# Tiles, exponentials and transfers of the mLSTM stage put in another order

## The chip, the cores and the metric

The kernel runs on one core of one Trainium2 chip. The time is the device time of one execution in microseconds (us). The program starts five instruction streams: PE (TensorE, the matmuls), DVE (VectorE), ACT (ScalarE), POOL (GpSimd) and SP (SyncE, which here only issues DMA transfers). They run at the same time and meet only at semaphores, so the time is set by whichever chain of work and waits is longest.

## The reference, cut to what matters

The program is two blocks of two layers each on 512 latent and 256 context tokens of 1024 features (768 tokens in all), in float32. The change lies in the first layer of the first block, an mLSTM mixer with 8 heads, run over chunks of 128 tokens in both directions:

```python
d = b[..., :, None] - b[..., None, :] + li[..., None, :]
d = jnp.where(jnp.tril(jnp.ones((L, L), dtype=bool)), d, -jnp.inf)
inter = b + m0[..., None]
m_t = jnp.maximum(jnp.max(d, axis=-1), inter)
wq = jnp.exp(d - m_t[..., None]) * jnp.einsum("bhctd,bhcsd->bhcts", q_c, k_c)
carry_w = jnp.exp(inter - m_t)
num = jnp.einsum("bhcts,bhcse->bhcte", wq, v_c) + carry_w[..., None] * jnp.einsum("bhctd,bhcde->bhcte", q_c, c0)
den = jnp.sum(wq, axis=-1) + carry_w * jnp.einsum("bhctd,bhcd->bhct", q_c, n0)
h = num / jnp.maximum(jnp.abs(den), jnp.exp(-m_t))[..., None]
```

Before it the tokens are projected to queries and keys, values, output gates and scan gates. Beside it every layer needs a modulation vector, `silu(c) @ ada_w + ada_b`, for the latents and for the context: 48 tiles of `ada_w` for this layer, of which the first 16 are done by matmuls at the start and the other 32 beside the projections.

## The kernel before, in words

**Weight stream.** All weights are read as tiles of 128x1024 floats (512 KB). `weight_plan` lists them in one order. SP loads tile i into one of three stage buffers; it waits until the tile three places earlier has been used up. A projection tile is then split into a rounded part and a remainder: `W.hi` lets ACT write the rounded part (L195), `W.lo` lets DVE subtract it (L209, `wlo`). There are four pairs of such parts, so ACT may round tile n+4 only when PE has used tile n. PE takes a tile in 24 matmuls of 512 and 24 of 256 columns, with the rounded part, the rounded part again against the remainder of the tokens, and the remainder. A modulation tile (`ada0`) takes no PE: DVE multiplies it with a spread conditioning vector (`CB0`, two of them) and sums, in two passes (L491), and only then is its stage buffer free. Where modulation tiles stand in the plan thus decides when DVE does these passes: it works in the order of the plan.

**The projections of this layer.** In the order of the plan: 1 tile of scan gates (`mgate`), 8 of queries and keys (`mqk`), 8 of values (`mv`, in two groups of four), 8 of output gates (`mo`), 8 of the output (`mout`). The results lie in four slots of PSUM, used in turn. A group of `mv` fills three slots and claims all three before its first matmul; ACT and DVE empty them (`mV`, L899 and L1018), DVE after the tiles that stand in the plan up to its place. After the first `mqk` tiles DVE works out the scans of the gates (L973 to L1009), some 25 us in one piece.

**The mixer.** Heads are taken in four pairs p = 0 to 3, each in two directions d. The names used below are those of the code:

- `spread_max(p)` is two DMA issues of ACT's queue that spread the rows of running maxima over 128 partitions, into `mD` (the tiles mDD[p][0] and mDD[p][1], 768 KB each). mDD[1] and mDD[3] share one place, the second half of `Ht`; `CB0` lay in that place too.
- `bands(p)` is two POOL instructions (L1138) that subtract the causal mask in `mD`.
- `decay(p, d)` is 12 exponentials of ACT over `mD` (L860), then DVE `weights(p, d)` multiplies the scores of PSUM into it (L1026).
- `spread_reach(p)` is four DMA issues (192 KB each) into `mRQ`; `ends(p)` copies the chunk ends to `mG` on ACT (L868); `reach(p)` is two POOL multiplications with the queries (L1145).
- PE: `keys` (turns the keys), `scores`, `states` (key-value products), `within(p, d)` (inside a chunk), `past(p, d)` (from the carried state; it waits for `reach(p)` and for DVE's state chain at L1056 and L1060).
- `sizes(p, d)` on ACT takes the absolute value of the denominators (`mDN`, L919) after `past(p, d)`; DVE `normalise(p, d)` takes their maximum with the floor (L1068), the reciprocal (L1070) and scales the result into `mH` (L1079 for d=0, L1085 for d=1); ACT `squares` and DVE `head_norm` (L1095) follow.

PE does, for each p: within(p,0), past(p,0), keys(p+1), within(p,1), past(p,1), the turning of the former pair, scores(p+1), states(p+1,0), states(p+1,1). The scores of the next pair need the PSUM slots that the result of direction 1 holds, so they wait for DVE's last L1085 of this pair.

Two orders are written out by hand and matter here: ACT's in the loop over p, and POOL's list of bands and reaches.

## Time and profile before

| what | value |
|---|---|
| median of 3 runs | 3561.91 us (3559.08 to 3564.73) |
| profiled execution | 3561.91 us, its span in the trace 3560.2 us |
| PE busy | 3242.3 us, 91% of the span |
| DVE, ACT, POOL busy | 1881.3, 1170.2, 208.9 us |
| DMA | 318.73 MB, mean 90 GB/s |

The span is the time from the first to the last instruction in the trace; 1.7 us of the profiled execution lie around it. The chain of the page is the work that ended last, followed back step by step. The mLSTM layer takes the first tenth: its projections run from 80 to 307 us, its pairs from 307 to 405 us.

### The profile page before, as it was taken

To read this page: it belongs to the slowest core of one execution; us is meant where nothing else is said; L and a number is where in the kernel's file an instruction comes from. 1 tells how busy PE (TensorE), PEld (TensorE's weight loads), DVE (VectorE), ACT (ScalarE), POOL (GpSimd) and SP (SyncE) were. 2 spreads that over 40 slices of the span, in tenths; PEclk is the share of its full clock that TensorE was granted. 3 is DMA by queue.
4 is the path that set the end of the run, shared out by engine and by line. 5 is a ranking of instruction groups with operands and counts; after the bars stand their busy time and mean duration, and the time that the engine had idled before them with its cause. 6 is when DMAs were issued, how large, how long until landed. Compare 5 with 4: busy or idle time off the path is not lost.

```text
span 3560.2 us, 44175 instructions
## 1 busy us (share of the span) xinstructions
PE 3242.3 (91%) x18456; PEld 2699.3 (76%) x18456; DVE 1881.3 (53%) x2747; ACT 1170.2 (33%) x1757; POOL 208.9 (6%) x144
## 2 busy tenths in 40 slices
PE   8998889999989779999998999988998888997997
PEld 8877778888877667777777878756887777775776
DVE  2765646655434664777454342574434544456543
ACT  3315331212232554222342333253212534425322
POOL 0002100000010000000001220000001012000001
PEclk9999999999989999999999999999999799989997
DMA  4454113333212002555221123102122222310321
GB/s 177 136 180 146 45 48 126 123 130 119 95 54 70 3 1 95 177 177 177 95 93 70 64 71 113 42 1 80 54 72 89 76 68 86 112 58 9 100 87 59
DMA packets 90926, 318.73 MB, mean 90 GB/s; under 512 B 10006, under 2 KB 11926, under 8 KB 89960
## 3 DMA queue, kind: packets, MB, share of 16 engines
q1 hardware_dynamic: 81348, 288.91, 24.5%
q10 hardware_dynamic: 9380, 26.99, 2.1%
q8 instruction: 147, 2.41, 0.3%
q14 instruction: 51, 0.42, 0.0%
HBM read 294.12 MB, written 21.74 MB: 89 GB/s over the span
## 4 chain that ended last, share of the span: by engine, by line
PE 78%; DVE 10%; ACT 8%; issue 4%; DMA 0%; ACTq 0%; POOL 0%; POOLq 0%; DVEq 0%; SPq 0%
PE PS L384 77%; ACT whi L195 2%; ACT Pq L1246 1%; DVE STs L1283 1%; PE PS L387 1%; ACT nt L588 1%; DVE JUNK L491 1%; DVE stage L491 1%; DVE STq L1283 1%; ACT Ps L1246 1%; DVE wlo L209 1%; ACT U L593 0%; DVE fg L693 0%; ACT Ht L2276 0%; ACT FS L1637 0%
## 5 line engine op out<-in xcount | busy, mean ns | idle before, releaser
L384 PE MATMUL PS<-U,whi 128*128 128x512 f32 (+1 forms) x5408 | 1176.7, 363 | 89.3 <-DVE U L613 24.1
L384 PEld LDWEIGHTS PS<-U,whi 128*128 128x128 f32 x5408 | 912.3, 192 | 278.0 <-issue 54.1
L209 DVE TENSOR_TENSOR wlo<-stage,whi 128x1024 fp32r<-128x1024 f32 x339 | 417.6, 1233 | 1107.8 <-ACT whi L195 1107.2
L195 ACT ACTIVATE whi<-stage 128x1024 fp32r<-128x1024 f32 x339 | 358.4, 1058 | 1459.3 <-PE PS L384 1424.5
L384 PE MATMUL PS<-U,wlo 128*128 128x512 f32 (+1 forms) x2704 | 621.4, 356 | 0.0
L384 PE MATMUL PS<-Y,whi 128*128 128x512 f32 (+1 forms) x2240 | 581.7, 363 | 18.3 <-DVE Y L695 12.2
L384 PEld LDWEIGHTS PS<-U,wlo 128*128 128x128 f32 x2704 | 458.5, 190 | 80.0
L384 PEld LDWEIGHTS PS<-Y,whi 128*128 128x128 f32 x2240 | 396.5, 191 | 93.1 <-DVE Y L695 14.2
L384 PE MATMUL PS<-Y,wlo 128*128 128x512 f32 (+1 forms) x1120 | 367.2, 362 | 0.0
L384 PE MATMUL PS<-whi,U 128*128 128x512 f32 (+2 forms) x832 | 237.2, 374 | 11.3 <-DVE mV L1018 6.4
L384 PEld LDWEIGHTS PS<-Y,wlo 128*128 128x128 f32 x1120 | 208.6, 190 | 34.9
L384 PEld LDWEIGHTS PS<-whi,U 128*128 128x128 f32 x832 | 158.5, 206 | 39.9 <-issue 11.9
L491 DVE CUSTOM_DVE_ANT_0 JUNK<-stage,CB,CL 128x1024 f32<-128x1024 f32 x128 | 163.7, 1279 | 0.5 <-DMA stage<-in_ada 0.4
L491 DVE CUSTOM_DVE_ANT_0 stage<-stage,CB,CL 128x1024 f32<-128x1024 f32 x128 | 164.0, 1281 | 0.0
L384 PE MATMUL PS<-wlo,U 128*128 128x512 f32 (+2 forms) x416 | 155.2, 373 | 0.0
L528 POOL TENSOR_TENSOR ACC<-ACC,SQ 128x768 f32<-128x768 f32 (+1 forms) x24 | 37.6, 1567 | 1356.3 <-ACT SQ L521 1356.3
L675 ACT ACTIVATE Y<-fg 128x768 fp32r<-128x768 f32 (+1 forms) x64 | 47.3, 739 | 207.7 <-DVE fg L693 207.7
L384 PEld LDWEIGHTS PS<-wlo,U 128*128 128x128 f32 x416 | 85.9, 206 | 12.8
L1246 ACT ACTIVATE Pq<-PS,STq 128x768 f32<-128x768 f32 (+1 forms) x80 | 65.1, 815 | 86.8 <-DVE STq L1287 67.8
L2312 POOL TENSOR_TENSOR ACC<-ACC,Ht 128x768 f32<-128x768 f32 (+1 forms) x14 | 21.8, 1561 | 1101.8 <-DVE Ht L2294 1101.8
L695 DVE TENSOR_TENSOR Y<-fg,Y 128x768 fp32r<-128x768 f32 (+1 forms) x64 | 52.8, 826 | 51.6 <-ACT Y L675 51.6
L1283 DVE TENSOR_REDUCE STq<-PS 128x1 f32<-128x768 f32 (+1 forms) x80 | 67.6, 845 | 16.9 <-PE PS L384 15.6
(408 smaller groups left out, 3329.3 us busy)
## 6 DMA issues: line engine op xcount, KB each, us to landing
stage<-in_w SPq DMA_DIRECT2D x128, 512.0 KB, 3.3
stage<-in_ada SPq DMA_DIRECT2D x80, 512.0 KB, 3.3
stage<-in_adb SPq DMA_DIRECT2D x48, 512.0 KB, 3.3
stage<-in_p_mg SPq DMA_DIRECT2D x16, 512.0 KB, 3.3
stage<-in_p_ma SPq DMA_DIRECT2D x16, 512.0 KB, 3.4
stage<-in_p_ms SPq DMA_DIRECT2D x16, 512.0 KB, 3.4
stage<-in_wo SPq DMA_DIRECT2D x16, 512.0 KB, 3.3
GS<-FS ACTq DMA_DIRECT2D x20, 384.0 KB
```

The costliest lines, as they stand in the source:

```text
L195: act.activation(self.parts[r % n][0], self.stage[i % len(self.stage)], ACT.Copy).then_inc(*self.S.up("w_hi", i))
L209: dve.tensor_tensor(lo, self.stage[i % len(self.stage)], hi.bitcast(F32), ALU.subtract).then_inc(*self.S.up("w_lo", i))
L384: return pe.matmul(o, l, r, start=start, stop=stop_, skip_group_check=True)
L387: return pe.transpose(o, i, IDENT[0:k, 0:k])
L491: dve.tensor_tensor_reduce(tile if v else JUNK, tile, CB[n][v], 1.0, col(("ada2_b" if b else "ada_b") + str(L), t), ALU.mult, ALU.add, MOD ...
L528: pool.tensor_tensor(ACC[:, 0:N], ACC[:, 0:N], SQ[k % 2][:, 0:N], ALU.add).then_inc(*up("sq_add", r, k))
L588: ins = act.activation(a[:, lo:hi], a[:, lo:hi], ACT.Identity, bias=mod(L, ish, k, v), scale=MU[:, 8 * v + k:8 * v + k + 1])
L675: act.activation(Y[:, 0, k, 0:N], FB[n % 2][:, 0:N], ACT.Copy).then_inc(*up("f_hi", L, g, k))
L695: dve.tensor_tensor(Y[:, 1, k, 0:N], b, Y[:, 0, k, 0:N].bitcast(F32), ALU.subtract).then_inc(*up("f_lo", L, g, k))
L1246: act.activation(a.P[n % 2][:, h, 0:c], B.of(("a_s", a.tag, n, h))[:, 0:c], ACT.Exp, bias=nm[:, h:h + 1], scale=0.125, accum_out=sm[:, h:h ...
L1283: dve.tensor_reduce(mx[:, h:h + 1], B.of(("a_s", a.tag, n, h))[:, 0:c], AX.X, ALU.max).then_inc(*up("a_max", a.tag, n, h))
L2312: pool.tensor_tensor(ACC[:, 0:N], ACC[:, 0:N], HT[:, k, 0:N], ALU.add).then_inc(*up("e_add", L, k))
```

## The change: what it does

1. `weight_plan`: the 32 modulation tiles stand earlier. Before, one stood behind each of `mqk` 3 to 7, two behind an `mv` tile (one behind the fourth and the eighth), and 13 among the `mo` tiles. Now two stand behind each of `mqk` 3 to 7 and behind each `mv` tile, and two behind each of `mo` 0 to 2; behind `mo` 3 to 7 none.
2. `CB0` lies in another place, under the last output gates (`mO` 5 to 7). So the second half of `Ht` is free as soon as the normalisation has read it, and `spread_max(1)` is issued right behind `spread_max(0)`, between the two groups of `mv`; the eviction of `mo` 5 waits for the last modulation tile.
3. ACT, `mqk` and `mo`: the rounding of a coming tile (`W.hi`) stands ahead of the eviction of the tile just projected.
4. ACT, exponentials: both directions of a pair stand together, for pair 0 behind `mo` 4, for pair p+1 between `sizes(p, 0)` and `ends(p + 1)`; before, direction 1 stood behind `sizes(p, 1)`.
5. POOL: `bands(3)` stands ahead of `reach(2)`.

```diff
--- before.py
+++ after.py
@@ -260,13 +260,13 @@
     add("mgate", [0])
     for j in range(8):
         add("mqk", [j])
-        ada(1 if j >= 3 else 0)
+        ada(2 if j >= 3 else 0)
     for j in range(8):
         add("mv", [j])
-        ada(1 if j % 4 == 3 else 2)
+        ada(2)
     for j in range(8):
         add("mo", [j])
-        ada(2 if j < 6 else 7 - j)
+        ada(2 if j < 3 else 0)
     add("mout", range(8))
     for L in range(2):
         if L:
@@ -435,7 +435,7 @@
 
 
         CB = [[place(f"CB{n}{v}", [128, 1024], F32, o + 4096 * v)[:, :] for v in range(2)]
-              for n, o in enumerate((offH + 12288, offZ + 16384, offZ + 16384))]
+              for n, o in enumerate((offY2 + 16384, offZ + 16384, offZ + 16384))]
         FIRST = [place(f"first{g}", [128, 2, 1024], F32, (offU + 8192 * g) if g < 6 else offY + 8192 * (g - 6))
                  for g in range(8)]
         JUNK = place("JUNK", [128, 1024], F32, offZ + 34848)[:, :]
@@ -851,14 +851,15 @@
                         *dma(f"m_rin{p % 2}", p, d, h))
 
         def act_mlstm(act):
-            def decay(p, d):
-                act.wait_ge(*at("m_band", p, d))
-                for h in range(2):
-                    r = m_row(p, h, d)
-                    for c in range(6):
-                        x = mDD[p][d][:, h, 128 * c:128 * c + 128]
-                        ins = act.activation(x, x, ACT.Exp, bias=maT[:, c, r:r + 1], scale=-1.0)
-                    ins.then_inc(*up("m_dx", p, h, d))
+            def decay(p):
+                for d in range(2):
+                    act.wait_ge(*at("m_band", p, d))
+                    for h in range(2):
+                        r = m_row(p, h, d)
+                        for c in range(6):
+                            x = mDD[p][d][:, h, 128 * c:128 * c + 128]
+                            ins = act.activation(x, x, ACT.Exp, bias=maT[:, c, r:r + 1], scale=-1.0)
+                        ins.then_inc(*up("m_dx", p, h, d))
 
             def ends(p):
                 act.wait_ge(*at(f"m_rin{p % 2}", p, 1, 1))
@@ -875,10 +876,10 @@
             act.activation(mTM[r40, :], mTM[r40, :], ACT.Ln).then_inc(*up("m_gexp", 1))
             for j in range(8):
                 i = T("mqk", j)
+                W.hi(act, i)
                 act.wait_ge(*at("w_used", i))
                 act.activation(mQK[:, j, :], B.of(i)[:, 0:TOK], ACT.Copy, scale=1.0 if j < 4 else 0.125).then_inc(
                     *up("m_qk", j))
-                W.hi(act, i)
             act.wait_ge(*at("m_rows"))
             act.activation(mRR[r40, :], mRR[r40, :], ACT.Exp, scale=-1.0).then_inc(*up("m_reach"))
             act.dma_start(mROWS[0, :, :], mMR[r40, :]).then_inc(*dma("m_spill", 0))
@@ -900,18 +901,19 @@
                                    rows_of(("mv", g), c, 512).rearrange("p (h e) -> p h e", e=128), ACT.Copy).then_inc(
                                        *up("m_va", g, c))
                 if g == 0:
+                    act.wait_ge(*at("n_mul", 0, 7))
                     act.wait_ge(*at("m_spill", 1))
                     spread_max(act, 0)
+                    spread_max(act, 1)
             for j in range(8):
                 i = T("mo", j)
+                W.hi(act, i)
                 act.wait_ge(*at("w_used", i))
+                if j == 5:
+                    act.wait_ge(*at("mod", T("ada0", 47), 1))
                 act.activation(mOT[:, j, :], B.of(i)[:, 0:TOK], ACT.Sigmoid).then_inc(*up("m_o", j))
-                W.hi(act, i)
-                if j in (3, 4):
-                    decay(0, j - 3)
-                if j == 6:
-                    act.wait_ge(*at("mod", T("ada0", 47), 1))
-                    spread_max(act, 1)
+                if j == 4:
+                    decay(0)
 
             def sizes(p, d):
                 act.wait_ge(*at("m_av", p, d))
@@ -939,11 +941,9 @@
             for p in range(4):
                 sizes(p, 0)
                 if p < 3:
-                    decay(p + 1, 0)
+                    decay(p + 1)
                     ends(p + 1)
                 sizes(p, 1)
-                if p < 3:
-                    decay(p + 1, 1)
                 if p < 2:
                     spread_reach(act, p + 2)
                 if p == 1:
@@ -1138,20 +1138,16 @@
                     pool.tensor_tensor(x, x, CM[:, 384 + 128 * d:512 + 128 * d].unsqueeze(1).to_broadcast([128, 12, 128]),
                                        ALU.subtract).then_inc(*up("m_band", p, d))
 
-            def reach(p):
+            bands(0)
+            bands(1)
+            for p in range(4):
                 for d in range(2):
                     x = mRQ[p % 2][d]
                     pool.wait_ge(*at("m_g", p, d))
                     pool.tensor_tensor(x, x, mQK[:, p, :], ALU.mult).then_inc(*up("m_q", p, d))
-
-            bands(0)
-            bands(1)
-            reach(0)
-            bands(2)
-            reach(1)
-            reach(2)
-            bands(3)
-            reach(3)
+                if p in (0, 1):
+                    bands(p + 2)
+
 
 
 
@@ -2375,7 +2371,7 @@
             for L in range(2):
                 act_norm_mod(act, 2 * L, L, 0, True)
                 if L == 0:
-                    act_spread(act, 0, ("n_mul", 0, 7))
+                    act_spread(act, 0)
                     act_mlstm(act)
                 else:
                     act_swa(act)
```

In the order of ACT's instructions the loop over the pairs shows points 4 and 2. Below is pair 0 and the start of the next step, before the change; mD10 and mD11 are the tiles of pair 1 in direction 0 and 1, mG the ends, mDN the sizes, mRQ the reach, mJ the squares.

```order
L919 ACTIVATE mDN_108<-PS 128x6 x2
L860 ACT_TABLE_LOAD
L860 ACTIVATE mD10_118<-mD10_118,maT_105 128x128 x12
L868 ACTIVATE mG_110<-mRQ10_127 128x6
L868 ACTIVATE mG_110<-mRQ11_128 128x6
L919 ACTIVATE mDN_108<-PS 128x6 x2
L860 ACTIVATE mD11_119<-mD11_119,maT_105 128x128 x12
L850 DMA mRQ00_125<-mROWS 64x768 x2
L850 DMA mRQ01_126<-mROWS 64x768 x2
L929 ACTIVATE mJ_124,mSQ_109<-mH00_135 128x128 x6
```

And the same place of ACT after the change:

```order
L921 ACTIVATE mDN_108<-PS 128x6 x2
L861 ACT_TABLE_LOAD
L861 ACTIVATE mD10_118<-mD10_118,maT_105 128x128 x12
L861 ACTIVATE mD11_119<-mD11_119,maT_105 128x128 x12
L869 ACTIVATE mG_110<-mRQ10_127 128x6
L869 ACTIVATE mG_110<-mRQ11_128 128x6
L921 ACTIVATE mDN_108<-PS 128x6 x2
L850 DMA mRQ00_125<-mROWS 64x768 x2
L850 DMA mRQ01_126<-mROWS 64x768 x2
L931 ACTIVATE mJ_124,mSQ_109<-mH00_135 128x128 x6
```

The twelve exponentials of direction 1 have moved from behind the second mDN to ahead of it, and ahead of both mG. The same holds for pairs 2 and 3.

POOL's list from the reach of pair 0 on, before (mRQ00 and mRQ01 serve pairs 0 and 2, mRQ10 and mRQ11 pairs 1 and 3; mD2 and mD3 are the bands of pairs 2 and 3):

```order
L1145 TENSOR_TENSOR mRQ00_125<-mRQ00_125,mQK_100 128x768
L1145 TENSOR_TENSOR mRQ01_126<-mRQ01_126,mQK_100 128x768
L1138 TENSOR_TENSOR mD20_120<-mD20_120,CM_60 128x1536
L1138 TENSOR_TENSOR mD21_121<-mD21_121,CM_60 128x1536
L1145 TENSOR_TENSOR mRQ10_127<-mRQ10_127,mQK_100 128x768
L1145 TENSOR_TENSOR mRQ11_128<-mRQ11_128,mQK_100 128x768
L1145 TENSOR_TENSOR mRQ00_125<-mRQ00_125,mQK_100 128x768
L1145 TENSOR_TENSOR mRQ01_126<-mRQ01_126,mQK_100 128x768
L1138 TENSOR_TENSOR mD30_122<-mD30_122,CM_60 128x1536
L1138 TENSOR_TENSOR mD31_123<-mD31_123,CM_60 128x1536
```

After the change, from the reach of pair 1 on:

```order
L1147 TENSOR_TENSOR mRQ10_127<-mRQ10_127,mQK_100 128x768
L1147 TENSOR_TENSOR mRQ11_128<-mRQ11_128,mQK_100 128x768
L1138 TENSOR_TENSOR mD30_122<-mD30_122,CM_60 128x1536
L1138 TENSOR_TENSOR mD31_123<-mD31_123,CM_60 128x1536
L1147 TENSOR_TENSOR mRQ00_125<-mRQ00_125,mQK_100 128x768
L1147 TENSOR_TENSOR mRQ01_126<-mRQ01_126,mQK_100 128x768
```

The two mD3 instructions now stand ahead of the reach of pair 2 instead of behind it.

On DVE the place between the two groups of `mv` shows point 1. Before, from the remainder of the eighth `mv` tile (wlo_53) to the emptying of PSUM:

```order
L209 TENSOR_TENSOR wlo_53<-stage_50,whi_52 128x1024
L491 ISA JUNK,MOD_63<-stage_51,CB_73,CL 128x1024
L491 ISA MOD_63 128x1
L491 ISA stage_51,MOD_63<-stage_51,CB_74,CL 128x1024
L491 ISA MOD_63 128x1
L1018 COPY mV<-PS 128x4x128 x3
```

After:

```order
L209 TENSOR_TENSOR wlo_53<-stage_50,whi_52 128x1024
L491 ISA JUNK,MOD_63<-stage_51,CB_73,CL 128x1024
L491 ISA MOD_63 128x1
L491 ISA stage_51,MOD_63<-stage_51,CB_74,CL 128x1024
L491 ISA MOD_63 128x1
L491 ISA JUNK,MOD_63<-stage_49,CB_73,CL 128x1024
L491 ISA MOD_63 128x1
L491 ISA stage_49,MOD_63<-stage_49,CB_74,CL 128x1024
L491 ISA MOD_63 128x1
L1018 COPY mV<-PS 128x4x128 x3
```

One modulation tile more stands between that remainder and the copy.

## Rows read from the trace of the kernel before

**Rows 1.** The page, shares of the chain that ended last, by engine

```profile
PE 78%; DVE 10%; ACT 8%; issue 4%; DMA 0%; ACTq 0%; POOL 0%; POOLq 0%; DVEq 0%; SPq 0%
```

**Rows 2.** Waits of the first 700 us: total us, times, longest us

```profile
PE PS L384 <- DVE mH L1085: 12.0, 3, 5.7
```

**Rows 3.** Windows: length, busy per engine (instructions), TensorE clock, DMA share, GB/s

```profile
330.25:337.40 7.15, 6.63 (x64) 6.16 (x64) 3.49 (x8) 3.74 (x17) 3.36 (x2) 0.60 0.42 104
378.50:383.80 5.30, 3.96 (x64) 3.60 (x64) 5.16 (x10) 4.96 (x25) 0.00 (x0) 1.00 0.02 3
```

**Rows 4.** Timeline (start, duration, instruction, [idle before]): DVE, end of the gate scans

```profile
123.98 1.22 DVE L209 TENSOR_TENSOR wlo<-stage,whi 128x1024 fp32r<-128x1024 f32 x1
```

**Rows 5.** Timeline of PE: start of the fifth mqk tile, start of mv

```profile
127.49 3.90 PE L384 MATMUL PS<-U,whi 128*128 128x512 f32 x16
...
162.43 0.50 PE L384 MATMUL PS<-whi,U 128*128 128x512 f32 x1
```

**Rows 6.** Timeline of ACT: the rounding behind the last mqk eviction

```profile
162.00 1.05 ACT L195 ACTIVATE whi<-stage 128x1024 fp32r<-128x1024 f32 x1
```

**Rows 7.** Timeline of DVE between the two groups of mv

```profile
198.61 1.28 DVE L491 CUSTOM_DVE_ANT_0 JUNK<-stage,CB,CL 128x1024 f32<-128x1024 f32 x1
...
201.13 1.89 DVE L1018 COPY mV<-PS 128x512 f32<-128x512 f32 x3
```

**Rows 8.** Timeline of PE: start of the second group of mv

```profile
202.70 1.19 PE L384 MATMUL PS<-whi,U 128*128 128x512 f32 x2 [6.42 <-DVE mV L1018]
```

**Rows 9.** Timeline of all engines, from the last projection to pair 0

```profile
304.95 6.86 POOL L1138 TENSOR_TENSOR mD<-mD,CM 128x1536 f32<-128x1536 f32 x2 [91.92 <-DMA mD<-mROWS]
...
308.97 3.92 DVE L209 TENSOR_TENSOR wlo<-stage,whi 128x1024 fp32r<-128x1024 f32 x1 [3.73 <-ACT whi L195]
...
312.76 1.08 ACTq L844 DMA_DIRECT2D mD<-mROWS  x2
...
313.89 0.31 ACT L868 ACTIVATE mG<-mRQ 128x6 f32<-128x6 f32 x2 [4.96 <-DMA mRQ<-mROWS]
313.90 2.42 PE L384 MATMUL PS<-mV,mKH 128*64 128x129 f32 x40 [3.43 <-DVE mKH L1044]
...
317.24 1.39 PE L384 MATMUL PS<-mS,mRQ 64*128 64x129 f32 x20 [0.92 <-DVE mS L1060]
```

**Rows 10.** Timeline of all engines, pair 0

```profile
320.22 3.62 ACT L860 ACTIVATE mD<-mD,maT 128x128 f32<-128x128 f32 x12
...
323.24 6.82 POOL L1138 TENSOR_TENSOR mD<-mD,CM 128x1536 f32<-128x1536 f32 x2 [5.47 <-DMA mD<-mROWS]
...
324.64 0.24 ACT L919 ACTIVATE mDN<-PS 128x6 f32<-128x6 f32 x2 [0.60 <-PE PS L384]
...
324.92 1.79 DVE L1068 TENSOR_TENSOR mDN<-mDN,meT 128x12 f32<-128x12 f32 x1 [0.96 <-ACT mDN L919]
...
327.01 3.19 DVE L1085 SCALAR_TENSOR_TENSOR mH<-PS,mDN,mH 128x128 f32<-128x128 f32 x12
```

**Rows 11.** Timeline of all engines, pair 1

```profile
348.09 1.30 DVE L1068 TENSOR_TENSOR mDN<-mDN,meT 128x12 f32<-128x12 f32 x1 [0.96 <-ACT mDN L919]
348.10 0.45 ACTq L850 DMA_DIRECT2D mRQ<-mROWS  x1
...
350.53 0.60 ACTq L844 DMA_DIRECT2D mD<-mROWS  x1
```

**Rows 12.** Timeline of all engines, pair 2

```profile
359.77 7.58 POOL L1138 TENSOR_TENSOR mD<-mD,CM 128x1536 f32<-128x1536 f32 x2 [8.65 <-DMA mD<-mROWS]
...
362.80 1.39 PE L384 MATMUL PS<-mS,mRQ 64*128 64x129 f32 x20
...
369.58 3.57 POOL L1145 TENSOR_TENSOR mRQ<-mRQ,mQK 128x768 f32<-128x768 f32 x2 [2.22 <-ACT mG L868]
...
374.52 0.24 ACT L919 ACTIVATE mDN<-PS 128x6 f32<-128x6 f32 x2 [4.92 <-PE PS L384]
...
378.52 1.61 PE L384 MATMUL PS<-mQK 64*128 64x128 f32 x24 [2.59 <-DVE mH L1085]
```

## The prediction

> **What bounds the kernel now.** I read the page's chain first [rows 1]: TensorE ends last and carries 78% of the chain, so a change counts only where it makes PE wait or stop waiting, plus the clock PE is granted. Next the waits of the first 700 us, the part that the change touches. Among the pairs PE's largest waits are for DVE's last scaling of a pair's result, three in all [rows 2]: scores of the next pair need its PSUM. Third, the timeline between 94 and 405 us. The projections leave PE almost no idle time; the one large gap is 6.42 us between the two groups of value tiles [rows 8]. The pairs are a tight ring PE, ACT, DVE, POOL, in which nearly any delay reaches PE. So I sum the gaps place by place, in the profiled execution's own time, which is the median itself: 3561.91 us. After the mixer the work is the same, and a shift carries through.
>
> **Queries and keys.** Behind the fourth tile stand two modulation tiles instead of one, and DVE does both before the 25 us of scans. A tile costs DVE 2.4 to 2.5 us (198.61 to 201.13) [rows 7]. The next remainder starts at 123.98 and lasts 1.22 [rows 4]; with 2.4 more it ends at 127.6, PE wants it at 127.49 [rows 5]: +0.2 us (bounds 0 and 1). Later tiles have DVE work of 1.2 + 2 x 2.4 = 6.1 us per tile against PE's 8.4 (127.49 to 135.9), so the lag closes.
>
> **Rounding ahead of eviction.** The rounding, 1.05 us, began at 162.00 right behind the last mqk eviction [rows 6]; now it precedes it, and the eviction ends near 163.1. The first value group claims the slot it frees and began at 162.43 [rows 5]: +0.7 us (0 to 1). Elsewhere four slots give a tile's eviction at least 8 us of slack, which covers 1 us.
>
> **Between the value groups.** DVE empties PSUM behind one modulation tile, now behind two: the gap of 6.42 us becomes 8.8. The tile's load has landed, since its buffer came free early. +2.4 us, bounds 2.3 and 2.6. It is the surest term.
>
> **Last projection to pair 0.** What speaks for the change is here. POOL's bands for pair 1 ran 304.95 to 311.8, because CB0 held their memory until late; DVE's remainder at 308.97 took 3.92 us instead of 1.2, it ended 1.1 us after POOL, and PE lost 3.43 us [rows 9]. With the bands a hundred us earlier that cover is gone, and something else is late next: mG comes at 313.89, after its DMA issues, and DVE's state chain and POOL's reach both wait for it. The chain then takes 0.2 + 0.3 + 1.5, PE can do past(0,0) near 316.1 instead of 317.24 [rows 9]. So -1.1 us, not -3.4 (the bounds: 0 if the mout load, which now comes earlier, delays the reach transfers; -3.4 if mG is not late). The moved bands may hold DVE at 213 to 221 us; cover is the remainder it then makes, for a tile that PE takes 20 us later.
>
> **Pair 0.** ACT now does 24 exponentials ahead of sizes(0,1). Twelve take 3.62 [rows 10]. From past(0,0) at 317.5: 0.3 sizes, 1.3 table, 7.2 exponentials, 0.3 mG, so sizes(0,1) ends at 326.8; before it was 324.9 [rows 10]. Then comes the maximum at L1068, two operands in SBUF. Before, it was issued at 324.92 while POOL ran the first band, and took 1.79 us, until that band ended at 326.63: it waits for the POOL instruction that is running. Now it is ready when the second band runs. That band ended at 330.06 [rows 10] and will end some 1.3 us earlier, because the mout load no longer shares its transfer: 328.8. Scaling starts at 329.2 instead of 327.01, and scores(1) at +2.2 against before, a term of +3.3 over the -1.1. Bounds: +1.2 if DVE slips in free, +4.6 if the band ends as before. I take the middle since pair 3's transfer, with no mout load beside it, let POOL start 9.2 us after its issue (350.53 to 359.77) [rows 11, 12], pair 2's 10.5 us after (312.76 to 323.24) [rows 9, 10].
>
> The Trainium skill, "SBUF — State Buffer", section "SBUF: two separate sides", says that DVE with two SBUF inputs and a GpSimd instruction exclude each other for the whole instruction, and that whoever starts first holds the ports. The row of 1.79 us agrees. By that rule DVE's modulation passes would be held beside the moved bands too, which no row of before shows; it would change nothing in the sum as long as the 20 us above hold.
>
> **Pair 1.** The same exponentials put sizes(1,1) 3.5 us later against the rest of the pair. Before, L1068 lost 1.30 us at 348.09 to POOL's reach(2) [rows 11]; that reach now comes later and this loss goes. Net 3.5 less 1.2 to 1.3: +2.3 us (bounds 1.5 and 3.6).
>
> **Pair 2.** POOL does bands(3) before reach(2). bands(3) can't start before their transfer lands, 359.77, and end at 367.4 [rows 12]. Against that clock past(2,0) stood at 362.80 and would now be ready at 365.1; but its reach can start only near 367.5, waits once for DVE's head_norm, and takes 1.8 (half of 3.57): ready at 369.4. Then ACT: sizes(2,0) at 371.6, 1.3 + 7.2 + 0.3, sizes(2,1) at 380.7, and it was 374.52. POOL's reach(3), released by the same mG, holds L1068 for another 1.5. Scores(3) come at 386.0 instead of 378.52 [rows 12]: +7.4 in all, of which 2.3 is pair 1's, so +5.1. Bounds: -0.2 if the reach is not late at all (then sizes(2,1) comes at 375.3), +6.8 if the transfer lands 1.7 us later.
>
> **Clock.** Scores and states of pair 1, after 5.7 us without a matmul, took 7.2 us at a granted clock of 0.60; those of pair 3, after a gap of 2.6, took 5.3 at 1.00 [rows 3]. The two levels are 1.2 and 2.4 GHz. Pair 3 will now follow a gap of some 6 us: +1.9 us (0 to 1.9).
>
> **Sum.** 0.2 + 0.7 + 2.4 - 1.1 + 3.3 + 2.3 + 5.1 + 1.9 = +14.8 us; 3561.9 + 14.8 = 3576.7, say 3576.5 us, +0.4%. With all lower values (-3.4 included) it is +1.4, with all upper ones +21.5.
>
> **Rivals.**
> First, reach(2) isn't late: the transfer of pair 3 lands before PE comes to past(2,0), or PE is late enough anyway. For it: it is the only term that hangs on a transfer's landing time. Against: it landed 9 us after its issue [rows 11, 12], and nothing moves the issue ahead. Then pair 2 gives -0.2: 14.8 - 5.3 = +9.5, 3571.4, or 3569.5 if the clock holds too.
>
> Second, not slower: the exponentials of direction 1 find room on ACT (idle 4.9 us at 374.52 [rows 12]) and PE keeps the whole 3.43 us of the collision. Place: sizes(p,1); it decides whether its result comes before DVE has finished scaling direction 0, near 323 us for pair 0. Price: 0.2 + 0.7 + 2.4 - 3.4 = -0.1, 3561.8 us. Against it: ACT was idle only 0.60 us ahead of that instruction in pair 0 [rows 10], where 3.6 us are put in.
>
> Third, pair 3's transfer is issued later. Before, the issue at 348.10 came while twelve exponentials stood ahead of it on ACT [rows 11], so ACT's sequencer runs at least that far ahead; now it must pass 16 instructions. If it can't, four to six more exponentials at 0.3 us delay the issues, up to 1.7 us in pair 2: 3578.2 us. The Trainium skill, "Advanced Engine Details and Errata", section "Engine Queue Depths", gives ScalarE 8 entries, by which this case would be certain; the row of 348.10, with twelve, speaks against a limit of 8, not against one of 12 to 15.
>
> Fourth, the weight stream starves: three loads per tile instead of two in mqk. If each took 4.3 us one after the other, a tile would need 12.9 against 8.4, and four tiles cost 18 us: 3595. Against: in the value group three loads per 8.4 us already ran with PE never waiting inside it.
>
> **Chances.** Forecast 0.55, reach not late 0.17, not slower 0.08, later issue 0.15, starving 0.05. The range 3566 to 3581 holds the forecast, the third rival, the first, and leaves out the second and the fourth and a mis-sized rest, about 2 in 10. A measurement of this kernel can tell 0.2%, 7.1 us, from no change. Slower than 3569.0: the forecast, the third and fourth and half of the first, 0.83; within 0.2%: the second and the rest of the first, 0.14; faster 0.03.
>
> **What would show it.** Step by step: the PE gap before the second value group 8.8 us; PE idle before mv 0.7; a DVE remainder near 309 us of 1.2 us; L1068 of pair 0 direction 1 issued 2 us later against past(0,0) and taking about 2 us; POOL's reach of pair 2 behind bands(3) and PE waiting for POOL 4 us at past(2,0); scores(3) after a gap over 6 us at clock 0.5 to 0.6. The time of everything behind the mixer should be the old one. The prediction is wrong if ACT's second set of exponentials does not delay the sizes, or if past(2,0) starts within 1 us of keys' readiness.

## The result, and the profile after

| kernel | median (executions) | lowest to highest | ratio to before, 95% interval |
|---|---|---|---|
| before | 3563.32 us (4) | 3559.08 to 3570.19 | |
| after | 3590.39 us (4) | 3577.8 to 3594.3 | 1.0074, 1.0051 to 1.0097 |

The change makes the kernel 0.74% slower, about 27 us, where 14.6 had been forecast; the time lies outside the range given. The profiled execution of after took 3578.54 us (span 3576.9), which is one of its shortest (ten executions of it on record lie at 3577.8 to 3596.1), so I read the trace place by place and not by its end.

The waits of PE in the first 700 us, after (columns as in [rows 2]):

```profile
PE PS L384 <- DVE mH L1085: 19.0, 3, 6.8
```

The three waits of [rows 2] have grown from 12.0 to 19.0 us. The largest new wait is not among the pairs. Timeline of PE after, starts of the two value groups, answering to [rows 5] and [rows 8]:

```profile
174.28 1.19 PE L384 MATMUL PS<-whi,U 128*128 128x512 f32 x2 [11.54 <-ACT mQK L881]
...
218.83 1.19 PE L384 MATMUL PS<-whi,U 128*128 128x512 f32 x2 [8.81 <-DVE mV L1018]
```

PE waits 11.54 us for the eviction of the last query/key tile, where it had waited for nothing. The gap between the groups is 8.81, as forecast. Timeline of ACT in the same stretch, answering to [rows 6]:

```profile
158.43 1.06 ACT L195 ACTIVATE whi<-stage 128x1024 fp32r<-128x1024 f32 x1 [5.14 <-DMA stage<-in_mv]
159.40 0.80 ACT L881 ACTIVATE mQK<-PS 128x768 f32<-128x768 f32 x1
165.50 1.06 ACT L195 ACTIVATE whi<-stage 128x1024 fp32r<-128x1024 f32 x1 [5.31 <-DMA stage<-in_mv]
166.46 0.79 ACT L881 ACTIVATE mQK<-PS 128x768 f32<-128x768 f32 x1
172.27 1.06 ACT L195 ACTIVATE whi<-stage 128x1024 fp32r<-128x1024 f32 x1 [5.01 <-DMA stage<-in_mv]
173.23 0.79 ACT L881 ACTIVATE mQK<-PS 128x768 f32<-128x768 f32 x1
```

The 1.06 us of a rounding is not the price. Each rounding waits for a load, and the loads now land 6.8 to 7.1 us apart. The rounding at 172.27 belongs to the fourth value tile, which PE wants 25 us after the start of the group; before, the same rounding came at 162.00 [rows 6], behind the eviction. Now the eviction at 173.23, which PE wants at 162.7, stands behind it.

Windows after, first half of the first value group (columns as in [rows 3]):

```profile
155.00:175.00 20.00, 8.46 (x60) 7.44 (x59) 17.80 (x28) 6.23 (x7) 0.00 (x0) 0.75 0.72 232
175.00:200.00 25.00, 25.00 (x102) 20.09 (x101) 16.40 (x25) 4.19 (x7) 0.00 (x0) 0.93 0.57 178
```

Behind the gap PE runs at a lower granted clock; the group takes 35.7 us (174.28 to 210.02) instead of 33.9 (162.43 to 196.28). From the last projection to pair 0, all engines, after, answering to [rows 9]:

```profile
324.60 1.23 DVE L209 TENSOR_TENSOR wlo<-stage,whi 128x1024 fp32r<-128x1024 f32 x1 [3.72 <-ACT whi L195]
...
325.85 0.33 SPq L184 DMA_DIRECT2D stage<-in_mout  x1
...
332.90 0.31 ACT L869 ACTIVATE mG<-mRQ 128x6 f32<-128x6 f32 x2 [7.63 <-DMA mRQ<-mROWS]
...
335.19 2.52 PE L384 MATMUL PS<-mS,mRQ 64*128 64x129 f32 x20 [5.93 <-DVE mS L1060]
```

The remainder takes 1.23 us, the collision is gone as forecast. But mG comes 9.34 us behind the first reach issue (323.56); in before it was 6.62 (307.27 to 313.89). Pair 0 after, answering to [rows 10]:

```profile
339.30 5.07 ACT L861 ACTIVATE mD<-mD,maT 128x128 f32<-128x128 f32 x17
340.29 6.82 POOL L1138 TENSOR_TENSOR mD<-mD,CM 128x1536 f32<-128x1536 f32 x2 [3.53 <-DMA mD<-mROWS]
340.88 2.89 DVE L1068 TENSOR_TENSOR mDN<-mDN,meT 128x12 f32<-128x12 f32 x1
...
346.53 0.21 ACT L921 ACTIVATE mDN<-PS 128x6 f32<-128x6 f32 x2
346.77 0.38 DVE L1068 TENSOR_TENSOR mDN<-mDN,meT 128x12 f32<-128x12 f32 x1 [0.76 <-ACT mDN L921]
```

The exponentials delay the sizes (346.53, 11.3 us behind past(0,0); 7.4 before). Beside POOL's bands the first maximum took 2.89 us, the second only 0.38; undisturbed it takes 0.17 to 0.18. Pair 2 after, answering to [rows 12]:

```profile
379.87 6.84 POOL L1138 TENSOR_TENSOR mD<-mD,CM 128x1536 f32<-128x1536 f32 x2 [29.23 <-DMA mD<-mROWS]
386.67 5.00 POOL L1147 TENSOR_TENSOR mRQ<-mRQ,mQK 128x768 f32<-128x768 f32 x2
389.24 1.77 PE L384 MATMUL PS<-mS,mRQ 64*128 64x129 f32 x20 [3.63 <-POOL mRQ L1147]
...
400.07 1.66 DVE L1068 TENSOR_TENSOR mDN<-mDN,meT 128x12 f32<-128x12 f32 x1 [3.40 <-ACT mDN L921]
405.28 2.93 PE L384 MATMUL PS<-mQK 64*128 64x128 f32 x24 [6.50 <-DVE mH L1085]
```

The reach runs behind bands(3), PE waits 3.63 us for it, and scores(3) come after a gap of 6.5 us. All as the prediction has it.

One thing moves the total and not the mixer. Windows of before and of after in the same tile of 144 narrow matmuls (128 columns each), far behind the mixer (first of before, then of after):

```profile
3155.00:3184.00 29.00, 29.00 (x136) 28.52 (x136) 4.53 (x5) 0.62 (x1) 0.00 (x0) 0.51 0.02 6
```

```profile
3183.00:3203.00 20.00, 18.16 (x150) 16.86 (x149) 7.22 (x6) 3.35 (x5) 0.00 (x0) 1.00 0.08 27
```

In both traces the tile starts behind a gap of 1.84 us. In the traced execution of before the granted clock then fell from 1.00 to about 0.5 of full (of 2.4 to 1.2 GHz) some 1.5 us into the tile, while PE was busy; in that of after it stayed at 1.00. The 144 matmuls took 29.3 us and 16.1 us. From DVE's reciprocal at 3079.67 to the last one at 3539.43 before has 459.8 us, after 444.5. That is 15.3 us which belong to the execution: a3 and c3 below, which differ from after only in or ahead of the mixer, have 459.7. So kernels are compared below by PE's times in the mixer. Medians of the total are given beside them, but they mix executions with and without this stretch of half clock.

### The profile page after: what moved, and what is told of

It reads as the page before. It is cut to its first block, busy times and chain, and to the rows that moved or that the text cites. A ratio compares the mean times of both kernels' runs of the same rounds, so it can differ in the third digit from the quotient of the medians.

```text
span 3576.9 us, 44174 instructions
## 1 busy us (share of the span) xinstructions
PE 3235.5 (90%) x18456; PEld 2692.7 (75%) x18456; DVE 1881.8 (53%) x2747; ACT 1167.2 (33%) x1755; POOL 209.6 (6%) x144
## 4 chain that ended last, share of the span: by engine, by line
PE 75%; DVE 10%; ACT 8%; issue 4%; DMA 1%; POOL 0%; ACTq 0%; POOLq 0%; DVEq 0%; SPq 0%
PE PS L384 74%; ACT whi L195 2%; DVE JUNK L491 1%; ACT Pq L1242 1%; DVE STs L1279 1%; DVE stage L491 1%; ACT nt L588 1%; PE PS L387 1%; DVE STq L1279 1%; DVE wlo L209 1%; ACT Ps L1242 1%; ACT mD L861 1%; ACT U L593 0%; DVE fg L693 0%; DMA stage<-in_ada 0%
## 5 line engine op out<-in xcount | busy, mean ns | idle before, releaser
L384 PE MATMUL PS<-whi,U 128*128 128x512 f32 (+2 forms) x832 | 224.7, 360 | 25.2 <-ACT mQK L881 11.5
L384 PEld LDWEIGHTS PS<-whi,U 128*128 128x128 f32 x832 | 148.5, 192 | 54.0 <-issue 14.3
L1279 DVE TENSOR_REDUCE STq<-PS 128x1 f32<-128x768 f32 (+1 forms) x80 | 67.6, 845 | 15.9 <-PE PS L384 14.6
```

The costliest lines, as they stand in the source:

```text
L384: return pe.matmul(o, l, r, start=start, stop=stop_, skip_group_check=True)
L1279: dve.tensor_reduce(mx[:, h:h + 1], B.of(("a_s", a.tag, n, h))[:, 0:c], AX.X, ALU.max).then_inc(*up("a_max", a.tag, n, h))
```

## The experiments

PE's times in us in each trace (n: executions behind the median): start of the value tiles, second value group, past(0,0), scores of pairs 1, 2 and 3, and the last pair's turning.

| kernel | values | group 2 | past(0,0) | scores 1 | scores 2 | scores 3 | last turning | median us (n) | ratio, 95% |
|---|---|---|---|---|---|---|---|---|---|
| before | 162.4 | 202.7 | 317.2 | 330.3 | 352.9 | 378.5 | 400.8 | | |
| after | 174.3 | 218.8 | 335.2 | 350.7 | 375.4 | 405.3 | 429.4 | 3590.4 (4) | 1.0074 |
| a1 | 167.3 | 212.5 | 328.0 | 345.0 | 369.7 | 400.2 | 424.2 | 3575.1 (6) | 1.0040 (1.0025-1.0055) |
| a2 | 173.3 | 217.6 | 332.9 | 348.1 | 369.0 | 400.4 | 422.6 | 3579.5 (6) | 1.0053 (1.0039-1.0067) |
| a3 | 174.6 | 218.9 | 334.7 | 351.5 | 377.2 | 403.3 | 426.9 | 3579.6 (6) | 1.0049 (1.0034-1.0064) |
| a4 | 163.4 | 205.1 | 319.6 | 332.4 | 355.0 | 380.5 | 402.7 | 3566.3 (11) | 1.0005 (0.9996-1.0013) |
| b1 | 167.0 | 211.2 | 325.4 | 338.4 | 361.1 | 386.6 | 408.8 | 3574.4 (12) | 1.0025 (1.0006-1.0044) |
| b2 | 162.7 | 203.0 | 316.6 | 329.5 | 351.5 | 377.7 | 400.0 | 3561.6 (12) | 0.9994 (0.9978-1.0010) |
| b3 | 162.9 | 198.3 | 311.3 | 324.2 | 346.0 | 371.0 | 393.2 | 3555.5 (8) | 0.9971 (0.9960-0.9982) |
| b4 | 188.1 | 228.4 | 344.5 | 356.1 | 377.9 | 402.8 | 425.7 | 3590.2 (6) | 1.0068 (1.0056-1.0081) |
| c1 | 163.1 | 198.5 | 310.4 | 323.9 | 345.8 | 370.3 | 392.5 | 3555.1 (12) | 0.9983 (0.9966-1.0001) |
| c2 | 168.1 | 212.9 | 327.7 | 342.9 | 365.0 | 389.9 | 412.8 | 3565.7 (12) | 1.0018 (0.9999-1.0038) |
| c3 | 173.8 | 218.8 | 333.4 | 350.0 | 374.1 | 401.4 | 425.0 | 3591.7 (6) | 1.0094 (1.0069-1.0119) |
| d1 | 162.8 | 212.6 | 327.0 | 340.7 | 363.4 | 388.6 | 410.9 | 3576.8 (12) | 1.0040 (1.0024-1.0056) |
| e1 | 162.3 | 202.9 | 319.3 | 332.5 | 355.2 | 380.9 | 403.1 | 3564.1 (12) | 0.9988 (0.9975-1.0002) |
| e2 | 167.1 | 204.8 | 317.2 | 330.6 | 353.3 | 378.3 | 400.5 | 3564.3 (11) | 0.9992 (0.9981-1.0004) |

The kernel before had medians of 3562.98 to 3565.82 beside them. The ratio is not that of the medians shown, and differs from it by up to 0.002 (c3: 1.0094, medians 1.0074). The traces of after, a1, a2, c2 and e1 are without the half clock near 3155 us (441 to 445 us between the two reciprocals), the others with it (457 to 460). In a1 to a3 four of six executions lie at 3571 to 3581 and two at 3585 to 3592, while none of the 17 of before beside them lies under 3560, so these medians flatter a1 to a3; c2's median equals that of before though its mixer is 12 us longer. Two traces of kernels that are alike up to a place differ there by 1 us or so (values in after, a2, a3: 173.3 to 174.6).

**a1, the order in the query/key tiles put back**

```diff
-                W.hi(act, i)
                 act.wait_ge(*at("w_used", i))
                 act.activation(mQK[:, j, :], ...)
+                W.hi(act, i)
```

> The kernel after, with ACT's eviction of each query and key tile back ahead of the rounding of a coming tile; in the output-gate tiles the rounding stays ahead. Theory A (the eviction of the last key tile stands behind a rounding that waits for a load, and the value tiles wait for that eviction): PE's first value matmul comes 9.5 to 11.5 us earlier, near 163 to 165 us instead of 174.3, and as PE has no 11.5-us gap there, its clock doesn't fall and 1.9 us more come back; the reciprocal behind the mixer near 498 us instead of 511.0, the time about 3577 against the median of after's 3590.4, ratio to the kernel before 1.004. Rival B (the weight loads are late for PE itself, whatever ACT's order): the gap only moves to a load, value tiles start at 173 to 174 us, time as after. Rival C (as predicted: the order costs 0.7 us): start at 173.6 us.

Value tiles start at 167.3, 6.95 us earlier: most of A, but not all. The last eviction still waits (4.38 us of PE), now behind the rounding of the third value tile at 165.32. The clock term did not come back: the first group took 36.3 us. Of the 6.95 us 5.3 are left at the last turning, because pair 0 took 17.0 us instead of 15.5. Timeline of DVE, a1:

```profile
339.63 1.84 DVE L1068 TENSOR_TENSOR mDN<-mDN,meT 128x12 f32<-128x12 f32 x1 [1.06 <-ACT mDN L921]
```

Here POOL does hold the second maximum, though not by a band: the bands had just ended (339.67), and the first reach of pair 1 ran from 339.63 on.

**a4, that order alone in the kernel before** (the diff of a1 turned round)

> The kernel before, with the one edit that in the query and key tiles ACT rounds a coming tile ahead of the eviction (point 3 of the change, first half); the plan of the weights is the old one, one modulation tile per projection tile. Theory A (order and plan cost only together: with one modulation tile the load of the tile that is rounded has landed by then): value tiles start 0.7 us later than before, at 163.1 us, ratio 1.000. Rival B (the order alone costs it): start at 172 to 174 us, ratio 1.003.

A holds: +0.93 at the value tiles. This is the 0.7 of the prediction, and it is the price only with the old plan. Behind it the first value group takes 35.4 us instead of 33.9.

**b1, the new places of the modulation tiles alone**

```diff
-        ada(1 if j >= 3 else 0)
+        ada(2 if j >= 3 else 0)
-        ada(1 if j % 4 == 3 else 2)
+        ada(2)
-        ada(2 if j < 6 else 7 - j)
+        ada(2 if j < 3 else 0)
```

> The kernel before with the new places of the modulation tiles only (point 1). All orders of ACT and POOL and the place of CB0 are the old ones. Theory A (the plan by itself makes the stage buffers late, since DVE closes two modulation tiles per projection tile and had 25 us of scans to catch up): value tiles start 4.9 us late as in the kernel with the eviction put back, the second group 9.8 us, ratio about 1.002 to 1.003. Rival B (as predicted): 0.2 us at the value tiles, 2.6 us at the second group, ratio 1.001. Rival C (the plan's later part, with fewer tiles beside the last projections, gives time back before pair 0): 9.8 us at the second group and less than 6 at the keys of pair 0.

A holds: +4.6 and +8.5 us (the 4.6, a first group that is 1.5 us longer, and 2.4 in the gap), +8.0 at the last turning. Nothing is given back later (C falls). B, my own step, falls.

**d1, b1 with the late rounding behind the last eviction**

```diff
-                W.hi(act, i)
+                if j != 6:
+                    W.hi(act, i)
```

> The kernel before with the new places of the modulation tiles, as b1, and one step of ACT moved: the rounding that stands behind the eviction of the seventh query/key tile comes behind that of the eighth, so that no rounding that waits for a late load stands ahead of the last eviction. Theory A (in b1 PE was not short of weights; ACT, which works in order, held an eviction back behind a rounding whose load was late): value tiles start 0 to 0.8 us after their time in the kernel before, at 162.4 to 163.2 us instead of 167.0; the second group +2.4 to 3.5 us, the last pair's turning about +3 instead of +8. Rival B (the weight stream itself is late for PE): the start stays at 166 to 167 us, or the wait comes back inside the value tiles.

Half of each: the value tiles start at 162.76, on time, but the second group at 212.55. Timeline of PE and of DVE, d1:

```profile
212.55 1.19 PE L384 MATMUL PS<-whi,U 128*128 128x512 f32 x2 [15.92 <-DVE mV L1019]
```

```profile
204.08 1.28 DVE L491 CUSTOM_DVE_ANT_0 stage<-stage,CB,CL 128x1024 f32<-128x1024 f32 x1
...
208.47 1.29 DVE L491 CUSTOM_DVE_ANT_0 JUNK<-stage,CB,CL 128x1024 f32<-128x1024 f32 x1 [3.11 <-DMA stage<-in_ada]
209.68 1.28 DVE L491 CUSTOM_DVE_ANT_0 stage<-stage,CB,CL 128x1024 f32<-128x1024 f32 x1
211.01 1.89 DVE L1019 COPY mV<-PS 128x512 f32<-128x512 f32 x3
```

The gap grew from 8.8 to 15.9. DVE's copies stand behind all passes up to the eighth value tile, and with the first group on time these passes, with the loads that they let out, set the start of the second: DVE waits 3.11 us for the last modulation load. In a1, b1 and c2 the second group starts at nearly the same time (211.2 to 212.9), but there 8.8 us behind the end of the first group, and in a1 and b1 the last two roundings of the stretch wait 7.34 us each for PE and not for a load; so DVE's stream had caught up, and a limit near 211 us is shown in d1 alone.

**e1, b1 with DVE's passes over half the columns** (it leaves out half of each product sum)

```diff
-    dve.tensor_tensor_reduce(tile if v else JUNK, tile, CB[n][v], 1.0,
+    w_ = 1024 if b or L else 512
+    dve.tensor_tensor_reduce((tile if v else JUNK)[:, 0:w_], tile[:, 0:w_], CB[n][v][:, 0:w_], 1.0,
```

> The kernel before with the new places of the modulation tiles, as b1, and both DVE passes of each modulation tile of this layer over 512 instead of 1024 columns (half of each product sum is left out, everything is loaded as before): a projection tile with two modulation tiles then costs DVE about 3.8 instead of 6.1 us. Theory A (DVE's passes set the pace: the roundings of b1 and of the kernel after came about 6.9 us apart since a buffer is closed only when DVE is through): the roundings catch up, value tiles start at 162.4 to 163.5 us instead of 167.0, the gap before the second group is about 6.4, and it starts at 203 to 204 us instead of 211.2. Rival B (the loads, three of 512 KB per tile, set the pace): roundings stay 6 us or more apart, the start stays at 165 to 167 us.

A holds. Timeline of ACT, e1; the roundings come 5.5 to 6.9 us apart from the start and catch up:

```profile
153.53 1.06 ACT L195 ACTIVATE whi<-stage 128x1024 fp32r<-128x1024 f32 x1 [5.15 <-DMA stage<-in_mv]
159.04 1.06 ACT L195 ACTIVATE whi<-stage 128x1024 fp32r<-128x1024 f32 x1 [3.76 <-DMA stage<-in_mv]
165.78 1.06 ACT L195 ACTIVATE whi<-stage 128x1024 fp32r<-128x1024 f32 x1 [3.80 <-DMA stage<-in_mv]
171.64 1.06 ACT L195 ACTIVATE whi<-stage 128x1024 fp32r<-128x1024 f32 x1 [1.37 <-DMA stage<-in_mv]
```

The same loads were there. So DVE's passes, which close the stage buffers, set the pace, together with the load that each closing lets out behind it: with DVE's work cut from about 6.1 to 3.8 us per tile, the mean distance of the roundings went only from 6.9 to 6.2 us, and ACT still waits for a load at each of them up to 171.64; so the loads stand close behind DVE.

**e2, b1 with the copies of each value group ahead of the passes**

```diff
-                for u in range(4):
+                for u in range(3):
                     W.hi(act, T("mv", 4 * g + u))
                 (the copies of the group)
+                W.hi(act, T("mv", 4 * g + 3))
```

and the same with DVE's `dve_lo`.

> The kernel before with the new places of the modulation tiles, as b1, and with ACT's and DVE's copies of each value group ahead of the rounding, the remainder and the two modulation tiles behind the group's last tile. Theory A (PE has its weights; only DVE's copy is late, standing behind passes that nobody needs yet): the gap before the second group becomes 1.6 to 2 us instead of 8.8 (1.6 in the version with one modulation tile), the group starts at 204 to 205 us, and the last pair's turning comes near its time in the kernel before. Rival B (the weight stream is late for PE at that point too): 3 us or more of waits appear at the following tiles.

A holds. Timeline of PE, e2:

```profile
204.75 0.70 PE L384 MATMUL PS<-whi,U 128*128 128x512 f32 x2 [1.58 <-DVE mV L1019]
```

The gap is 1.58 us and no wait comes behind it up to 300 us; the last turning is at 400.5, 0.3 us before that of the kernel before. That PE is short of weights is refuted. But the plan is not free: the value tiles still start at 167.1, the first group takes 36.1 us, and b3, which has the same order of copies with the old plan (and the other place of CB0), starts its second group 6.5 us earlier. The earlier copies gain about what the plan costs.

**a2, the exponentials of pairs 1 to 3 apart again**

```diff
-                    decay(p + 1)
+                    decay(p + 1, (0,))
                     ends(p + 1)
                 sizes(p, 1)
+                if p < 3:
+                    decay(p + 1, (1,))
```

> The kernel after, with the exponentials of the two directions of pairs 1 to 3 again apart (direction 1 behind the sizes of direction 1). Theory A (the second twelve exponentials delay the sizes, and through them the scores of the next pair): the step from the scores of one pair to those of the next was 24.7 and 29.9 us after the change; it gets 3.2 us shorter from pair 1 to 2 and 3.7 us from pair 2 to 3, where part of it is lost since POOL's reach of pair 2 is late anyway; nothing in pair 0, where the maximum at L1068 was held by POOL's second band until 347.1 anyway; scores(3) after a shorter gap, so perhaps 1.9 us of clock. Mixer 4 to 7 us shorter. Rival B (ACT had room for them, the pairs are set by POOL's list): 0 to 1 us.

A in its place: from scores 1 to scores 2 20.9 us against 24.7 after. From scores 2 to 3 it is 31.4 against 29.9, since PE now waits 9.39 us for POOL's reach; and behind the shorter gap of 3.03 us the clock term is back (5.3 us to within(3,0) instead of 7.2). Pair 0: 15.1 against 15.5, for POOL's bands still held both maxima (2.44 and 1.22 us). The last turning is 6.8 us earlier, of which 2.3 lay ahead of past(0,0), where the edit changes nothing.

**a3, the reach of pair 2 ahead of bands(3) again**

```diff
-                if p in (0, 1):
-                    bands(p + 2)
+                if p in (0, 2):
+                    bands(2 + p // 2)
```

> The kernel after, with POOL's reach of pair 2 back ahead of the bands of pair 3. Theory A (the reach stands behind bands that wait for their transfer): past(2,0) has no wait for POOL (3.63 us after the change) and all behind it comes 3.6 us earlier, scores(3) at about 401.7 instead of 405.3; mixer 3.1 to 4.1 us shorter, the rest unchanged. Rival B (POOL's reach would be held by other work, or past(2,0) waits for DVE's state chain instead): 0 to 1 us.

A holds: PE does past(2,0) without a wait, and scores 2 to 3 takes 26.2 us instead of 29.9. The last turning gained only 2.6, as this trace was 1.8 us later than after at scores 2, ahead of what it changes.

**c2, all three orders put back in the kernel after** (the diffs of a1, a2 and a3)

> The kernel after with all three orders put back together: eviction ahead of the rounding in the query/key tiles, exponentials of the two directions apart, reach of pair 2 ahead of bands(3). Points 1 and 2 and the order in the output-gate tiles remain. Theory A (the orders carry what is not the plan's): value tiles +4.6 to 4.9 us, keys of pair 0 +8.5 to 10.3, and from there the pairs take no more than 1 to 2 us longer than before, so the last pair's turning comes 9 to 12 us after its time in the kernel before, not 28.7. The single reversals gave 5.3, 6.8 and 2.6 us there, 14.7 together; theory A wants 17 to 20, since exponentials and reach hide one another in pair 2. Rival B (they are additive): +14.

A in the main (its +8.5 to 10.3 at the keys of pair 0 was missed by a little): +10.5 there, +12.0 at the last turning, 16.7 us less than after, where A wanted 17 to 20; the single ones add up to 14.6. With a scatter of 1 us or so between traces A and B lie too close to be told apart surely. The pairs take 1.5 us longer than before, 2.1 of it in pair 0, where POOL's bands held both maxima (2.45 and 1.22 us), and a little comes back.

**b2, the other place of CB0 alone**

```diff
-              for n, o in enumerate((offH + 12288, offZ + 16384, offZ + 16384))]
+              for n, o in enumerate((offY2 + 16384, offZ + 16384, offZ + 16384))]
```

with `spread_max(act, 1)` behind `spread_max(act, 0)` and the waits that go with it, as in point 2.

> The kernel before with the other place of CB0 only, so that the row maxima of direction 1 are spread between the two value groups (point 2). Theory A (as predicted): POOL's bands for pair 1 run near 215 us, DVE's remainder at 309 us takes 1.2 instead of 3.9, the products of pair 0 come without their wait of 3.43 us, but past(0,0) waits for mG: -1.1 us there; the rest follows it, -1 to -3.4 us in the mixer. Rival B (what made the fourth reach transfer of pair 0 late after the change, 1.7 us, lies in this point, not in the plan): 0 to +1.7 us at past(0,0).

past(0,0) comes 0.6 us earlier, 0.8 against the keys (forecast -1.1): mG is the next thing late, at 314.34. The total can't be told from no change. Beside a moved band, which POOL ran from 215.19 to 219.72, a modulation pass of DVE took 4.53 us instead of 1.28; PE had no wait from it. Timeline of DVE, b2:

```profile
216.26 4.53 DVE L491 CUSTOM_DVE_ANT_0 JUNK<-stage,CB,CL 128x1024 f32<-128x1024 f32 x1
```

**c3, the kernel after with the last early mout load held**

```diff
-            W.load(sp, T("mout", 6) + 1)
+            W.load(sp, T("mout", 5) + 1)
+            sp.wait_ge(*at("m_g", 0, 1))
+            W.load(sp, T("mout", 6) + 1)
```

> The kernel after with the one edit of c1: SP holds the last mout load ahead of pair 0 back until both mG are written. Theory A (the load is what made mG late in the kernel after, 9.3 us behind the first reach issue): mG 6.3 to 7 us behind the issue, past(0,0) 2.3 to 3 us earlier against the keys of pair 0, and the mixer shorter by 2 to 3 us. Rival B (something else in the plan or ACT's order makes the transfers slow): 8 to 9 us, no change.

Timeline of ACT, c3 (first reach issue at 323.81):

```profile
331.06 0.31 ACT L869 ACTIVATE mG<-mRQ 128x6 f32<-128x6 f32 x2 [5.54 <-DMA mRQ<-mROWS]
```

7.25 us instead of 9.34, and past(0,0) 2.1 us earlier against the keys: the load accounts for most of it. The mixer is 4.5 us shorter, more than that (PE's wait for the reach of pair 2 fell from 3.63 to 1.72), and the median 3591.7 does not show it: not told from no change.

**b3, meant to beat both: b2 with e2's copies first.**

> A version meant to beat both: the kernel before with the other place of CB0 (as b2), and with ACT's and DVE's copies of each value group ahead of the rounding, the remainder and the modulation tile that stand behind its last tile. Theory A (the gap of 6.42 us is the rounding 1.06, the remainder 1.2, one modulation tile 2.4 and the copies): the gap becomes about 2.0 us, and the clock behind it doesn't fall as far, up to 1.5 us more; with b2's gain 5 to 9 us at the mixer's end, ratio 0.998. Rival B (what is put behind the copies is late for the second group): 2 to 4 us of it come back as waits inside the second group.

PE's gap before the second group is 1.58 us where it was 6.42, no wait comes back, and the last turning is 7.5 us earlier, 6.7 us earlier than in b2. Ratio 0.9971 (0.9960 to 0.9982): faster than both kernels. The gain in the total is near the limit of what can be told: the interval of c1, whose mixer is shorter still, ends at 1.0001.

**c1, b3 with the load held as in c3**

> The version with the copies of each value group first and the other place of CB0, and SP holds the last load of an mout tile ahead of pair 0 back until both mG are written. Theory A (that load, which the shorter DVE remainder sets free 2.3 us earlier, shares the DMA engines with the eight reach transfers; in four traces where the remainder took 3.6 to 4.1 us mG came 6.5 to 6.7 us after the first reach issue, in six where it took 1.2 it came 6.9 to 9.3 us after it): mG 6.3 to 6.7 us after the issue instead of 7.7, past(0,0) about 1 to 1.2 us earlier against the keys of pair 0, mixer 1 to 2 us shorter. Rival B (the landing times only scatter, or the transfer of pair 2's rows is what is shared with): mG at 7 to 9 us, no gain.

mG 6.76 us behind the issue instead of 7.72, past(0,0) 0.96 us earlier against the keys: A. The last turning gained 0.7, which no median can tell: 3555.07 us against b3's 3555.48.

**b4, a bare shift**

```diff
+            for _ in range(30):
+                gate(dve.memset(mWR[r40, :], 0.0))
             dve.wait_ge(*at("m_gexp", 1))
```

> The kernel before with 30 dependent memsets of one DVE tile, about 0.92 us each, put among the gate scans: everything behind the fourth query/key tile comes later by 20 to 28 us, and nothing else differs. It asks what such a shift does to the tile of 144 narrow matmuls near 3155 us, which ran at half clock (33.1 us) in the traced execution of before and at full clock (19.8 us) in that of after. Theory A (a bare shift frees that tile from the slow clock in part of the executions, as in the kernels with the change): executions lie in two groups about 15 us apart, the lower one only 5 to 15 us over the kernel before. Rival B (the change itself frees it): one group, 20 to 30 us over before, the tile at half clock always.

The trace is 24.9 us late at the last turning and 30.9 at the reciprocal near 3080; the median is 3590.15, that of after. One of six executions lay at 3580, five at 3588 to 3593. In the kernel before, beside it, 4 of 25 lay at 3541 to 3551. So executions that are some 15 us shorter occur with the kernel before too, and neither theory holds as written: the change is not needed for them. Whether it makes them more or less frequent can't be settled with these numbers, and why the clock falls in one execution and not in another stays open.

## Why the prediction was wrong

The direction and the order of the pairs' terms were right; the size was not. That the profiled executions differ by only 16.6 us, near the 14.8 of the sum, is luck: it is 28.7 in the mixer, 3.4 more up to the reciprocal near 3080 us, and 15.3 back behind it. Terms in us, from the traces of before and after, up to the last turning:

| term | forecast | measured |
|---|---|---|
| queries/keys, and rounding ahead of eviction | +0.2, +0.7 | +11.9 |
| clock in the first value group | none | +1.9 |
| between the value groups | +2.4 | +2.4 |
| last projection to past(0,0) | -1.1 | +1.8 |
| pair 0 | +3.3 | +2.5 |
| pair 1 | +2.3 | +2.0 |
| pair 2 | +5.1 | +4.3 |
| clock of pair 3 | +1.9 | +1.9 |
| sum | +14.8 | +28.7 |

- **The step that failed** is "Rounding ahead of eviction": "+0.7 us (0 to 1)". I priced the rounding by its own 1.05 us, in the old plan, and took the four slots as slack; I had worked out DVE's lag two paragraphs up ("6.1 us per tile against PE's 8.4, so the lag closes") and never set the two side by side. PE's tiles were served, but ACT, in order, stood at a rounding four tiles ahead whose load was late. a4 has the order at +0.9, b1 the plan at +4.6, both together +11.9. Of the 13.9 us that the sum lacks, 12.9 are this term and the clock behind it, both priced from the old plan.
- **"The lag closes"** was right for PE's remainders, and too fast for the rest. From 126.3 us on DVE had a tile's work of 6.1 us plus waits, and the roundings came 6.9 us apart, not 6.1. So against PE's 8.4 they gained only 1.5 us per tile, and the rounding of the fourth value tile was still 10.3 us behind its time before. At the second group the lag had closed in after, a1 and b1 (gap 8.8 us, as forecast), at the price of the late first group; d1 shows what it costs where the first group is on time. e1 brings both groups near their old times by halving the passes, e2 the second by going round them.
- **Rivals.** The first two are refuted: PE waited 3.63 us for reach(2) (and a3 takes the wait away), and the kernel is slower. My fourth (loads of 4.3 us one after the other, PE starved in mqk) named the right stream and the wrong victim: PE was busy for 35.9 of the 36 us from 126 to 162 (before: 36.0). No row shows its 4.3 us; the page of before has 3.3 from issue to landing of such a load. That its 3595 lies nearer to the 3590.4 than my forecast is luck.
- **Clock.** Also the 11.5-us gap has the clock term that I gave to pair 3 only: a gap of PE is to be priced with what follows it. b1, a1 and a4 show 35.3 to 36.3 us for the first value group after gaps of 4.1, 4.4 and 0.9 us, before 33.9.
- **Last projection to pair 0.** I gave 0 as the upper bound should the mout load delay the reach transfers; it was +1.8. The collision on DVE had held that load back until 312.92, and so protected the transfers that mG waits for. In the seven traces with a remainder of 3.5 to 4.1 us (before, a4, b1, b4, d1, e1, e2) that load comes late, and mG 6.5 to 7.1 us behind the first reach issue. In those without the collision mG comes 6.9 (b2) to 9.3 us (after) behind it, and holding the load gives 6.8 (c1) and 7.3 (c3). These two ranges overlap; the medians of the eight transfers from issue to landing do not (3.6 to 4.0 us with the collision, 5.1 to 5.9 without, 4.0 and 4.1 with the load held), and c1 and c3, with one edit each, show that it is the load's doing. The Trainium skill, "SBUF — State Buffer", section "SBUF: two separate sides", was cited for collisions of this kind; by that rule, the trace agrees: beside the bands the remainder takes 3.92 us, with the bands gone 1.23. The prediction left open whether modulation passes are held too. They are: b2 has one of 4.53 us. As forecast, PE did not wait for it.
- **Pair 0, mechanism partly wrong.** The sizes were delayed as forecast, by 3.9 us, but the second maximum was hardly held (0.38 us against 1.79 before): 3.9 - 1.4 = +2.5. Instead the first took 2.89, which cost nothing, as DVE then still waited 0.76 us for ACT. Late mG had delayed past(0,0), so POOL's bands, which wait for their own transfer, began 5.1 us behind it and not 6.0. In c3 the second band held the second maximum as forecast (1.54 us), in a1 and a3 the reach right behind the bands did (1.84, 1.66), and the pair took 3.7 to 4.0 us longer than before; in a2 and c2, with the exponentials apart, the bands held both and it took 2.1 longer. So two causes overlap here, and undoing the exponentials alone gives back only 0.4.
- **Pairs 1 and 2, clock of pair 3** were right in mechanism and within 1 us. a2 and a3 confirm them one by one: without the exponentials pair 1 takes 3.8 us less, without the bands ahead of it the reach is on time.
- **Third rival** (a later issue of the transfers): small. After the change the reach rows of pair 2 were issued at 344.11, 0.2 us behind PE's past(0,1), with eleven instructions still to run on ACT (seven exponentials, two mG, two mDN); those of pair 3 at 368.98, 0.8 us behind past(1,1), where before it was 0.3. So half a microsecond at most came from there.
- **"Everything behind the mixer should be the old one"** failed in the profiled execution by 15.3 us, 13.2 of them the clock in the tile near 3155 us, and by 3.4 us the other way between the mixer and 3080 us, whose cause stays open (in the other traces that stretch differs from before by -1.7 to +7.1).

## What to carry to other kernels

An instruction moved ahead of another on an in-order engine costs its wait, not its duration: look for what it waits for in the changed kernel, and who waits for what is now behind it. When a stream is made denser, add up its closing engine's work over the whole stretch, and ask which urgent copy stands at its end; put such copies ahead of work that nobody needs yet (b3: 0.29% faster). And a stall that you remove may have been holding back a transfer.
